# One layer of a three-branch decoder on one core: key drains moved ahead of two convolutions, a transpose moved forward, gate scalars read from PSUM

## The chip, the cores and the metric

The kernel runs on one core of a Trainium2 chip. The time is device microseconds (us) of one execution; lower is better. The engines are TensorE (PE in the profile, its weight loads PEld), VectorE (DVE), ScalarE (ACT), GpSimd (POOL) and SyncE (SP), each with a queue of its own that it works off in order.

## The reference

One layer over 512 tokens of width 1024. A combined projection feeds three token mixers (A: sparse attention over the 128 keys that a topk over index scores picks; B: gated DeltaNet; C: compressed, selected and window attention), then gates, branch projections and the output projection. The change lies in B and in C's compressed keys:

```python
g = -jnp.exp(a_log) * jax.nn.softplus(a_in + dt_bias)
g_cum = jnp.cumsum(g, axis=-1)
decay = jnp.where(lower, jnp.exp(jnp.where(lower, g_cum[..., :, None] - g_cum[..., None, :], 0.0)), 0.0)
a_mat = jnp.where(strict, jnp.einsum('bnhid,bnhjd->bnhij', k * beta, k) * decay, 0.0)
t_inv = lax.linalg.triangular_solve(eye + a_mat, eye, left_side=True, lower=True)
kc = rms_norm(compress_blocks(k_cmp, cmp_pos[0], phi_w1[0], phi_w2[0]), k_norm[0])
```

q, k and v of B pass a causal convolution of four taps and SiLU first; q and k are normalised.

## The kernel before, in words

The kernel is written engine by engine, each queue by hand; semaphores tie them together. Order of the work: x is normalised and transposed; the input projection goes through ten chunks of w_in (C0, C1, A0, QI, A2, B0, B1, B3, B4, B2; `project`, L1683 to L1685, three f16 matmuls for each f32 product); then comes B's recurrence over four token chunks c = 0 to 3, then 48 attention units u, then branch and output projections. The six gate chunks (L1979 to L1983) are no stage: `fill(n)` puts n of their matmuls wherever TensorE would wait.

**Weights.** SyncE loads a chunk in pairs of rows into three stage buffers. ScalarE scales and rounds each (`hi_split`, L740 and L748), GpSimd subtracts for the low part (`lo_split`, L528, called by `follow`), and TensorE waits for the low part. A load waits for the low part that frees its stage.

**B's inputs.** B3 brings the decay gates; B2 is the v part (features 8 to 11). `conv(m)` on VectorE (L1256, three times L1258) convolves feature m, ScalarE applies SiLU, GpSimd squares features 0 to 7 for the norms. From the gates VectorE makes the log decays g_t (L1323 to L1327); TensorE sums them (L1948, L1949, bank "sums": per token and per chunk), and GpSimd multiplies them with a triangle (`cumulative_input`, L584) for the `cumulative` matmul (L1912, bank "gc"). VectorE copies the sums into gc_, gl_ and kd_s (L1335 to L1339), subtracts (`difference(0)`, L1366), ScalarE exponentiates (`decay_exp`, L895, L896), GpSimd makes three products (`masked_decays`, L592, L595, L598), for which it also needs `key_scales` (own_root at L1038 to L1045 on 32 columns, to L1352). `decayed_products(0)` (L1379, L1381) then drains the key products kk and qk (L1881, eight matmuls each), and the first product of the inverse is L1889.

**Compressed keys.** `compressed_keys` (L1275 to L1280) norms the 31 compressed keys with own_root on one column of 31 rows; TensorE transposes them (kcT, inside B2), `twin` (L1146, L1147) drains them.

**Banks.** VectorE's two PSUM banks (`V`) are used in turn, in the order of the list v_names, and a use waits until the one two places before it is drained:

```python
v_names += list(chain(*([("ak", h)] for h in range(A_HEADS)))) + ["cmpkv", "sq", "sqT", "sums"]
v_names += [("gc", 0), ("kk", 0), ("qk", 0), "kcT", ("n", 0)]
...
def free(self, name):
    return self.at[name] + 1 - len(self.banks)
```

"sq" and "sqT" hold the square sums and their transpose (L1719, behind ScalarE's copy L901). So kcT waits for the drain of kk.

**Topk.** 96 half rounds (MAX8 at L1289, MATCH_REPLACE at L1292) over 256, 384 and then 512 scores are spread over VectorE's queue by `rounds(n)` and `between_steps`; their result is first used in unit 32. Attention units take one each.

**Waits on the same engine.** `hold` makes an engine wait for its own instruction to finish.

## Time and profile before

| | us |
|---|---|
| median of 3 runs | 604.04 (603.85 to 605.86) |
| the profiled execution | 606.39 |
| its span | 604.5 |
| TensorE busy | 548.3 (91%) |
| VectorE busy | 388.2 (64%) |
| ScalarE busy | 322.2 (53%) |
| GpSimd busy | 221.1 (37%) |

Times within the profile are microseconds from the span's start. A row of a timeline has the start, the length, the engine, the line, what is written and read, and the idle time of the engine just before it with what ended it. Matmuls are pipelined, so that a row's length is more than the spacing to the next. A TensorE clock of 1.00 is 2.4 GHz, one of 0.50 is 1.2 GHz.

### The profile page before, as it was taken

How to read it: one execution, taken by the hardware profiler on the slowest of the kernel's cores; microseconds unless marked ns; L12 is line 12 of the kernel's file. 1: busy time of each engine (PE TensorE's matmuls, PEld its weight loads, DVE VectorE, ACT ScalarE, POOL GpSimd, SP SyncE). 2: the span in 40 equal slices, each digit the busy share in tenths (PEclk: the TensorE clock that was granted, in tenths of full speed). 3: DMA queues.
4: the chain of work that ended last, by engine and by line, in shares of the span. 5: the costliest groups of instructions: out<-in, count | busy, mean ns of one | idle time of the engine just before them, and what ended most of it. 6: DMA issues, size and time to landing. Idle time of an engine off the chain costs nothing.

```text
span 604.5 us, 10710 instructions
## 1 busy us (share of the span) xinstructions
PE 548.3 (91%) x4087; PEld 306.8 (51%) x4087; DVE 388.2 (64%) x920; ACT 322.2 (53%) x573; POOL 221.1 (37%) x164
## 2 busy tenths in 40 slices
PE   2999999999999848999899998989898998899997
PEld 1544556543457423566475665545555564333443
DVE  6521397765498696777867778578896664576311
ACT  4555745356567844542624523876767675345320
POOL 0154453522046742242730712432323463234420
PEclk9999999999999997999999999999999998999999
DMA  9346865644024420220220201211221212252411
GB/s 318 109 122 155 149 107 156 206 127 117 26 54 123 121 89 2 70 72 1 75 66 3 74 32 35 72 36 36 70 71 36 71 36 69 71 210 70 140 52 53
DMA packets 31173, 52.93 MB, mean 88 GB/s; under 512 B 2743, under 2 KB 13329, under 8 KB 31121
## 3 DMA queue, kind: packets, MB, share of 16 engines
q1 hardware_dynamic: 30825, 51.68, 29.9%
q10 hardware_dynamic: 296, 0.55, 0.5%
q8 instruction: 33, 0.54, 0.4%
q14 instruction: 19, 0.16, 0.1%
HBM read 49.80 MB, written 2.42 MB: 86 GB/s over the span
## 4 chain that ended last, share of the span: by engine, by line
PE 66%; DVE 19%; ACT 7%; issue 5%; SPq 2%; DMA 1%; POOL 0%; DVEq 0%; ACTq 0%; PEldq 0%; POOLq 0%
PE bank L1683 13%; PE bank L1685 11%; PE bank L1684 11%; PE bank L1979 5%; PE bank L1981 5%; PE bank L1889 5%; PE bank L1983 5%; PE bank L1881 3%; PE bank L1719 3%; ACT stage L740 2%; PE bank L1825 2%; DVE bank L1258 1%; DVE early L1292 1%; DVE small L1289 1%; ACT late L962 1%
## 5 line engine op out<-in xcount | busy, mean ns | idle before, releaser
L528 POOL TENSOR_TENSOR w_lo<-stage,w_hi 128x1024 f16<-128x1024 f32 (+4 forms) x76 | 149.5, 1971 | 226.3 <-ACT w_hi L748 226.2
L748 ACT ACTIVATE w_hi<-stage 128x1024 f16<-128x1024 f32 (+4 forms) x76 | 74.5, 981 | 14.2 <-PE bank L1685 9.2
L1979 PE MATMUL bank<-hT_hi,w_hi 128*128 128x512 f16 x192 | 73.0, 380 | 1.7 <-PE bank L1983 0.9
L740 ACT ACTIVATE stage<-stage,small 128x512 f32<-128x512 f32 (+4 forms) x120 | 73.6, 663 | 0.5 <-DMA stage<-in_w_in 0.5
L1981 PE MATMUL bank<-hT_lo,w_hi 128*128 128x512 f16 x192 | 72.9, 380 | 0.3
L1983 PE MATMUL bank<-hT_hi,w_lo 128*128 128x512 f16 x192 | 72.8, 379 | 0.3 <-PE bank L1685 0.2
L1683 PE MATMUL bank<-w_hi,hT_hi 128*128 128x260 f16 (+4 forms) x192 | 60.9, 317 | 3.3 <-DVE hT_lo L1066 1.4
L1685 PE MATMUL bank<-w_hi,hT_lo 128*128 128x260 f16 (+4 forms) x192 | 60.8, 316 | 0.0
L1684 PE MATMUL bank<-w_lo,hT_hi 128*128 128x260 f16 (+4 forms) x192 | 60.7, 316 | 0.0
L1683 PE MATMUL bank<-hT_hi,w_hi 128*128 128x512 f16 (+1 forms) x128 | 48.1, 376 | 2.5 <-ACT work L731 1.5
L1685 PE MATMUL bank<-hT_hi,w_lo 128*128 128x512 f16 (+1 forms) x128 | 47.8, 374 | 0.0
L1684 PE MATMUL bank<-hT_lo,w_hi 128*128 128x512 f16 (+1 forms) x128 | 47.8, 374 | 0.0
L1889 PEld LDWEIGHTS bank<-work 64*64 64x64 f32 x992 | 35.5, 134 | 22.7 <-issue 11.6
L1889 PE MATMUL bank<-work 64*64 64x64 f32 x992 | 42.0, 222 | 2.8 <-DVEq L1360 2.3
L962 ACT ACTIVATE late<-late,small 128x128 f32<-128x128 f32 (+3 forms) x48 | 26.8, 557 | 27.7 <-DVE small L1469 27.6
L1390 DVE COPY_PREDICATED work<-level_masks,bank 128x256 f32<-128x256 uint8 (+1 forms) x48 | 21.3, 443 | 17.4 <-PE bank L1719 9.0
L1683 PE MATMUL bank<-strips,w_hi 128*128 128x512 f16 x64 | 25.1, 392 | 4.4 <-DVE strips L1582 1.5
L1683 PEld LDWEIGHTS bank<-w_hi,hT_hi 128*128 128x128 f16 x192 | 18.7, 98 | 19.6 <-issue 6.0
L1258 DVE SCALAR_TENSOR_TENSOR bank<-qkvT,par,bank 128x512 f32<-128x512 f32 x36 | 27.2, 755 | 1.3
L1589 DVE TENSOR_TENSOR late<-bank,late 128x128 f16<-128x128 f32 (+3 forms) x48 | 23.2, 483 | 7.1 <-ACT late L983 6.9
L1289 DVE MAX8 small<-early 128x8 f32<-128x512 f32 (+2 forms) x46 | 25.8, 561 | 2.9
L1647 DVE SCALAR_TENSOR_TENSOR late<-bank,late 128x512 f32<-128x512 f32 x8 | 5.5, 691 | 33.9 <-PE bank L1685 33.9
(331 smaller groups left out, 1139.4 us busy)
## 6 DMA issues: line engine op xcount, KB each, us to landing
stage<-in_w_in SPq DMA_DIRECT2D x40, 512.0 KB, 3.7
stage<-in_c_phi_w SPq DMA_DIRECT2D x8, 512.0 KB, 4.0
stage<-in_w_branch SPq DMA_DIRECT2D x8, 512.0 KB, 3.9
stage<-in_w_out SPq DMA_DIRECT2D x8, 512.0 KB, 4.3
stage<-in_w_in SPq DMA_DIRECT2D x8, 260.0 KB, 2.8
strips<-rel_rows SPq DMA_DIRECT2D x8, 256.0 KB, 7.1
late<-in_x SPq DMA_DIRECT2D x1, 2048.0 KB, 9.1
out_x<-late SPq DMA_DIRECT2D x8, 256.0 KB, 2.0
```

Of the source, the lines that this page charges most:

```text
L528: gp.tensor_tensor(piece_view(w_lo[:, k % PAIRS, :], c), piece_view(stage[:, piece_at[c, j] % STAGES, :], c), piece_view(w_hi[:, k % PAIRS ...
L740: ins = nc.scalar.activation(full[:, r, :], full[:, r, :], ACT.Copy, scale=g_w[:, 2 * j + r:2 * j + r + 1])
L748: nc.scalar.activation(piece_view(w_hi[:, k % PAIRS, :], c), full, ACT.Copy).then_inc(hi_ready, 1)
L962: nc.scalar.activation(probs[u % 2][:, 0:L], probs[u % 2][:, 0:L], ACT.Exp, bias=nmx[:, u:u + 1], scale=1.0 / LOGIT_SCALE, accum_out=rsum[ ...
L1258: ins = ve.scalar_tensor_tensor(acc, qkvT[:, m, w:w + T], tap[w], acc, ALU.mult, ALU.add)
L1683: mm(ps, lhs[0], rhs[0], start=start, stop=False)
L1684: mm(ps, lhs[0], rhs[1], start=False, stop=False)
L1685: return mm(ps, lhs[1], rhs[0], start=False, stop=stop)
L1889: ins = mm(ps[o:o + HALF, h * HALF:(h + 1) * HALF], lhs(h, slice(r, r + HALF)), rhs(h, slice(r, r + HALF)), start=True, stop=True)
L1979: mm(G.bank(g)[:, :], w[0], h[0], start=k == 0, stop=False)
L1981: mm(G.bank(g)[:, :], w[0], h[1], start=False, stop=False)
L1983: ins = mm(G.bank(g)[:, :], w[1], h[0], start=False, stop=k == KC - 1)
```

## The change

- VectorE: the log decays go ahead of `compressed_keys`; gc_, gl_ and kd_s are read from the bank "sums", without a copy between; `key_scales` is cut in two and goes ahead of `difference(0)`; `decayed_products(0)` goes ahead of conv(9), conv(10) and seven of the rounds, directly behind conv(8); kcT's drain goes ahead of conv(8); conv(11) goes into the first level of the inverse. The rounds move: 2, then 3, 2, 2 here, none in the first level, and two instead of one at units u with u % 4 == 2.
- TensorE: the sums' matmuls go from behind B4's last tile to ahead of it, `cumulative(0)` from inside B2 to ahead of B2, kcT from B2's third tile to its first, the key products from behind B2's second tile to behind its first, the transposes of n from the fourth tile to the second. The bank list has kcT ahead of kk.
- ScalarE: the split of B2's first pair goes from behind the softplus to ahead of the eighth SiLU.
- GpSimd: the resets go ahead of `cumulative_input(0)`, the cmp_strip copies behind the splits that follow B2.

```diff
--- before.py
+++ after.py
@@ -57,7 +57,7 @@
 
 FILL_Z, FILL_U, FILL_X, FILL_T = 7, 2, 7, 3
 
-ROUNDS_IN, ROUNDS_LOG, ROUNDS_SUM, ROUNDS_ROOT, ROUNDS_CONV = 0, 1, 1, 1, (6, 4, 3)
+ROUNDS_IN, ROUNDS_LOG, ROUNDS_CONV = 0, 2, (3, 2, 2)
 
 Y_EARLY = {34: (4,), 36: (5,), 40: (6,), 42: (7,), 46: (2,), 47: (3,)}
 Y_ORDER = (4, 5, 6, 7, 2, 3, 0, 1)
@@ -266,7 +266,7 @@
         v_names += ["cq0", "cq1", "kcmp", "vcmp", "ckvT", "aq0", "aq1"]
         v_names += [("ukv", t) for t in range(NT)] + ["ks", "kw", "kiT"]
         v_names += list(chain(*([("ak", h)] for h in range(A_HEADS)))) + ["cmpkv", "sq", "sqT", "sums"]
-        v_names += [("gc", 0), ("kk", 0), ("qk", 0), "kcT", ("n", 0)]
+        v_names += [("gc", 0), "kcT", ("kk", 0), ("qk", 0), ("n", 0)]
         for c in range(NT):
             for l in range(1, LEVELS):
                 v_names += [("z", c, l)] + ([("u", c, l)] if l < LEVELS - 1 else []) + [("ut", c, l)]
@@ -357,7 +357,6 @@
         max8 = cols(16)
         beta_t, g_t, sp_a, sp_b, neg_exp_a, dt_b = cols(16), cols(16), cols(16), cols(16), cols(4), cols(4)
         rk, nk = cols(16), cols(16)
-        sums_sb = cols(32)
         mx, nmx, rsum = cols(48), cols(48), cols(48)
         cmx, crs = cols(16), cols(16)
         fac = cols(4)
@@ -613,12 +612,16 @@
                 for m in range(4):
                     squares_b(m + 4 * (c == CH_B3))
             follow(CH_B4, 0)
-            cumulative_input(0)
             gp.memset(t_invT, 0.0)
             reset(t_h)
             reset(t_hT)
+            cumulative_input(0)
             for t in range(1, 4):
                 follow(CH_B4, t)
+            masked_decays(0)
+            follow(CH_B2, 0)
+            follow(CH_B2, 1)
+            follow(CH_B2, 2)
 
             gp.wait_ge(strips_loaded, 16 * (P // ROW_COPIES))
             for q in range(NT):
@@ -626,10 +629,6 @@
                 first = 415 - P * q
                 ins = gp.tensor_copy(cmp_strip[:, :, q, 0:n], strips[:, A_HEADS:, first:first + 16 * (n - 1) + 1:16])
             ins.then_inc(cmp_strip_ready, 1)
-            masked_decays(0)
-            follow(CH_B2, 0)
-            follow(CH_B2, 1)
-            follow(CH_B2, 2)
 
             def scaled_output(c):
 
@@ -878,6 +877,7 @@
             silu_conv(2)
             drain_chunk(CH_B3, "B3", lambda t: raw_b[:, t, 0:260], 260, between=lambda t: silus(t, {0: (3,), 1: (4,), 2: (5,), 3: (6,)}))
 
+            hi_split(CH_B2, 0)
             silu_conv(7)
             drain(("B4", 0), raw_b[:, 0, 260:520], 260, scale=1.0 / W_SCALE)
             act.wait_ge(s_drained, S.filled(("B3", 3)))
@@ -895,7 +895,6 @@
                 hold(nc.scalar.activation(decay, decay, ACT.Relu, scale=-1.0))
                 nc.scalar.activation(decay, decay, ACT.Exp, scale=-1.0).then_inc(exp_ready, 1)
 
-            hi_split(CH_B2, 0)
             drain(("B4", 1), raw_b[:, 1, 260:520], 260, scale=1.0 / W_SCALE)
             act.wait_ge(v_filled, V.filled("sq"))
             nc.scalar.activation(sum_rows, V.bank("sq")[:, :], ACT.Copy).then_inc(v_drained, 1)
@@ -1316,7 +1315,6 @@
             hold(ve.scalar_tensor_tensor(sp_b, sp_a, -1.0, sp_a, ALU.mult, ALU.max))
             hold(ve.tensor_scalar(sp_a, sp_a, 0.0, None, ALU.max))
             ve.nop().then_inc(GATE_IN.sem, 1)
-            compressed_keys()
             rounds(ROUNDS_LOG)
             GATE_OUT.wait(ve, "sp")
             for g in (beta_t, raw_c1[:, :, 192:204]):
@@ -1326,17 +1324,15 @@
             hold(ve.tensor_tensor(gt, sa, neg_exp_a.unsqueeze(1).to_broadcast([P, NT, 4]), ALU.mult))
             hold(ve.tensor_scalar(g_t, g_t, -1.0, None, ALU.mult))
             ve.nop().then_inc(gsum_ready, 1)
-            rounds(ROUNDS_SUM)
-            rounds(ROUNDS_ROOT)
+            compressed_keys()
             ve.tensor_copy(ss_b.rearrange("p (a t h) -> p t h a", a=2, t=NT),
                            filled("sqT")[:, :].rearrange("p (t h n) -> p t h n", t=NT, h=4)[:, :, :, 0:2]).then_inc(v_drained, 1)
             ve.wait_ge(v_drained, V.filled("sqT"))
             ps = filled("sums")
-            ve.tensor_copy(sums_sb, ps[:, 0:32]).then_inc(v_drained, 1)
+            hold(ve.tensor_copy(gc_, ps[:, 0:16]))
+            ve.tensor_copy(gl_, ps[:, 16:32])
+            ve.tensor_tensor(kd_s, ps[:, 16:32], gc_, ALU.subtract).then_inc(v_drained, 1)
             ve.wait_ge(v_drained, V.filled("sums"))
-            ve.tensor_copy(gc_, sums_sb[:, 0:16])
-            ve.tensor_copy(gl_, sums_sb[:, 16:32])
-            hold(ve.tensor_tensor(kd_s, sums_sb[:, 16:32], sums_sb[:, 0:16], ALU.subtract))
             ve.nop().then_inc(GATE_IN.sem, 1)
 
             def key_scales():
@@ -1347,6 +1343,8 @@
                 hold(ve.tensor_tensor(a_s, beta_t, rk, ALU.mult))
                 hold(ve.scalar_tensor_tensor(n_s, a_s, -1.0, rk, ALU.mult, ALU.mult))
                 ve.nop().then_inc(scales_ready, 1)
+
+            def decay_scales():
                 GATE_OUT.wait(ve, "exps")
                 ve.tensor_scalar(negegc, egc, -1.0, None, ALU.mult)
                 hold(ve.tensor_tensor(kd_s, ekd, rk, ALU.mult))
@@ -1468,18 +1466,18 @@
                 ve.wait_ge(v_drained, V.filled(("lg", m, q, h)))
                 ve.tensor_scalar(nmx[:, u:u + 1], mx[:, u:u + 1], -1.0 / LOGIT_SCALE, None, ALU.mult).then_inc(logits_ready, 1)
 
+            key_scales()
             difference(0)
-            key_scales()
+            twin("kcT", kcT[:, 0, 0:N_CMP], kcT[:, 1, 0:N_CMP], R_CK, N_CMP)
+            decay_scales()
+            conv(8)
+            decayed_products(0)
             rounds(ROUNDS_CONV[0])
-            conv(8)
+            level_zero(0)
             rounds(ROUNDS_CONV[1])
             conv(9)
-            decayed_products(0)
-            twin("kcT", kcT[:, 0, 0:N_CMP], kcT[:, 1, 0:N_CMP], R_CK, N_CMP)
             rounds(ROUNDS_CONV[2])
-            level_zero(0)
             conv(10)
-            conv(11)
             for c in range(NT):
                 norm = output_norm(c - 1) if c else iter(())
                 softmax = compressed_softmax() if c == NT - 1 else iter(())
@@ -1487,6 +1485,9 @@
 
                 def between_steps(l, late_in_level=False):
 
+                    if (c, l, late_in_level) == (0, 1, False):
+                        conv(11)
+                        return
                     if l < 3 or next(extras, "end") == "end":
                         rounds(1)
                         if not late_in_level:
@@ -1601,7 +1602,7 @@
                     for _ in norm:
                         pass
                 elif u < 28:
-                    rounds(1)
+                    rounds(2 if u % 4 == 2 else 1)
                 for f in Y_EARLY.get(u, ()):
                     y_lo(f)
                 if u % 4 == 3 and u >= 7:
@@ -1942,23 +1943,22 @@
                 if t == 2:
                     pe.wait_ge(v_drained, V.filled("sq"))
                     transposes("sqT", [sum_rows[:, t * P:(t + 1) * P] for t in range(NT)])
-                if t == 3:
                     pe.wait_ge(gsum_ready, 1)
                     ps = v_bank("sums")
                     mm(ps[:, 0:16], tri, g_t, start=True, stop=True)
                     mm(ps[:, 16:32], ones[:, :], g_t, start=True, stop=True).then_inc(v_filled, 1)
+                if t == 3:
+                    cumulative(0)
 
             def between_b2(t):
-                if t == 1:
+                if t == 0:
                     key_products(0)
 
             def within_b2(t, k):
                 if (t, k) == (0, 2):
-                    cumulative(0)
-                if (t, k) == (2, 1):
                     T_IN.wait(pe, "kc")
                     transposes("kcT", [raw_c0[0:N_CMP, 0, 0:128]], N_CMP)
-                if (t, k) == (3, 1):
+                if (t, k) == (1, 6):
                     GD.wait(pe, ("nnt", 0))
                     transposes(("n", 0), [neg_nT[:, h, :] for h in range(4)])
```

Line numbers of the changed kernel are one to three lower on VectorE from L1289 on, and one higher on TensorE. Three places, before and after, each as the queue has them.

TensorE, from the transposes of the square sums (sqT) to the first matmuls of B2. Before, the last rows of B4 and the first of B2:

```order
L1684 MATMUL bank<-w_lo,hT_hi 128x260
L1685 MATMUL bank<-w_hi,hT_lo 128x260
L1948 MATMUL bank<-small,consts 128x16
L1949 MATMUL bank<-small,ones 128x16
L1683 MATMUL bank<-hT_hi,w_hi 128x512
L1684 MATMUL bank<-hT_lo,w_hi 128x512
L1685 MATMUL bank<-hT_hi,w_lo 128x512
L1683 MATMUL bank<-hT_hi,w_hi 128x512
```

Now:

```order
L1686 MATMUL bank<-w_hi,hT_lo 128x260
L1720 MATMUL bank<-consts,early 128x128 x4
L1948 MATMUL bank<-small,consts 128x16
L1949 MATMUL bank<-small,ones 128x16
L1684 MATMUL bank<-w_hi,hT_hi 128x260
L1685 MATMUL bank<-w_lo,hT_hi 128x260
```

and at B4's end:

```order
L1685 MATMUL bank<-w_lo,hT_hi 128x260
L1686 MATMUL bank<-w_hi,hT_lo 128x260
L1913 MATMUL bank<-work,ones 128x512
L1684 MATMUL bank<-hT_hi,w_hi 128x512
L1685 MATMUL bank<-hT_lo,w_hi 128x512
L1686 MATMUL bank<-hT_hi,w_lo 128x512
L1684 MATMUL bank<-hT_hi,w_hi 128x512
```

L1948 and L1949 are the sums; they stood behind B4 and are now ahead of its last tile. L1913 is the cumulative matmul (L1912 before), now the first thing behind B4.

VectorE, from the end of the key scales to the first copies for the inverse. Before:

```order
L1256 TENSOR_SCALAR bank<-qkvT,par 128x512
L1258 SCALAR_TENSOR_TENSOR bank<-qkvT,par,bank 128x512 x3
L1292 MATCH_REPLACE early<-small,early 128x256
L1289 MAX small<-early 128x8
L1292 MATCH_REPLACE early<-small,early 128x256
L1289 MAX small<-early 128x8
L1256 TENSOR_SCALAR bank<-qkvT,par 128x512
L1258 SCALAR_TENSOR_TENSOR bank<-qkvT,par,bank 128x512 x3
L1379 TENSOR_TENSOR work<-bank,late 128x512
L1381 TENSOR_TENSOR work<-bank,work 128x512
L1390 COPY_PREDICATED work<-level_masks,work 64x256 x2
L1146 TENSOR_SCALAR kcT<-bank,par 128x31
```

Now:

```order
L1364 TENSOR_TENSOR work<-bank,g_scale 128x512
L1145 TENSOR_SCALAR kcT<-bank,par 128x31
L1146 SCALAR_TENSOR_TENSOR kcT<-bank,par,kcT 128x31
L1349 TENSOR_SCALAR g_scale<-g_scale 128x16
L1350 TENSOR_TENSOR g_scale<-g_scale,small 128x16
L1255 TENSOR_SCALAR bank<-qkvT,par 128x512
L1257 SCALAR_TENSOR_TENSOR bank<-qkvT,par,bank 128x512 x3
L1377 TENSOR_TENSOR work<-bank,late 128x512
L1379 TENSOR_TENSOR work<-bank,work 128x512
L1388 COPY_PREDICATED work<-level_masks,work 64x256 x2
L1288 MAX small<-early 128x8
```

L1379 and L1381 (now L1377 and L1379) are the key drains, L1256 and L1258 (L1255, L1257) one convolution, L1146 (L1145) the drain of kcT. Two convolutions and ten rounds stood ahead of the key drains, now one convolution does, and kcT is drained ahead of it.

GpSimd, from the split of B2's first pair on. Before:

```order
L528 TENSOR_TENSOR w_lo<-stage,w_hi 128x1024
L584 TENSOR_TENSOR work<-consts,small 128x512
L617 MEMSET work 128x512
L587 COPY work<-consts 128x256 x2
L528 TENSOR_TENSOR w_lo<-stage,w_hi 128x1024 x3
L627 COPY cmp_strip<-strips 128x4x7
L627 COPY cmp_strip<-strips 128x4x15
L627 COPY cmp_strip<-strips 128x4x23
L627 COPY cmp_strip<-strips 128x4x31
L592 TENSOR_TENSOR work<-work,consts 128x512
L595 TENSOR_TENSOR late<-work,g_scale 128x512
L598 TENSOR_TENSOR work<-work,small 128x512
```

Now:

```order
L527 TENSOR_TENSOR w_lo<-stage,w_hi 128x1024
L615 MEMSET work 128x512
L586 COPY work<-consts 128x256 x2
L583 TENSOR_TENSOR work<-consts,small 128x512
L527 TENSOR_TENSOR w_lo<-stage,w_hi 128x1024 x3
L591 TENSOR_TENSOR work<-work,consts 128x512
L594 TENSOR_TENSOR late<-work,g_scale 128x512
L597 TENSOR_TENSOR work<-work,small 128x512
L527 TENSOR_TENSOR w_lo<-stage,w_hi 128x1024 x4
L630 COPY cmp_strip<-strips 128x4x7
```

L584 (L583) is the cumulative input, L592 to L598 (L591 to L597) are the masked decays, L528 (L527) the splits. The cumulative input now stands behind the resets, the masked decays directly behind B2's splits.

## Rows read from the trace of the kernel before

**Rows 1.** the page, part 4: the chain that ended last, shares by engine
```profile
PE 66%; DVE 19%; ACT 7%; issue 5%; SPq 2%; DMA 1%; POOL 0%; DVEq 0%; ACTq 0%; PEldq 0%; POOLq 0%
```

**Rows 2.** windows: length, each engine's busy time (instructions), granted clock, DMA share, GB/s
```profile
200.00:220.00 20.00, 17.95 (x101) 9.85 (x98) 15.20 (x38) 16.63 (x25) 15.78 (x17) 1.00 0.37 106
220.00:240.00 20.00, 11.39 (x43) 4.99 (x44) 13.88 (x29) 5.16 (x9) 3.39 (x2) 0.74 0.19 53
```

**Rows 3.** TensorE's timeline: start us, length us, engine, line, operation, [idle before <-releaser]
```profile
199.38 0.66 PE L1719 MATMUL bank<-consts,early 128*128 128x128 f32 x4 [1.77 <-ACT early L901]
...
205.73 1.02 PE L1912 MATMUL bank<-work,ones 128*128 128x512 f32 x2
...
209.24 0.39 PE L1683 MATMUL bank<-hT_hi,w_hi 128*128 128x512 f16 x1 [0.55 <-POOL w_lo L528]
...
218.59 0.38 PE L1685 MATMUL bank<-hT_hi,w_lo 128*128 128x512 f16 x1
...
228.61 0.28 PE L1719 MATMUL bank<-consts,early 31*128 31x31 f32 x1 [9.64 <-DVE work L1379]
...
234.22 0.38 PE L1684 MATMUL bank<-hT_lo,w_hi 128*128 128x512 f16 x1
...
236.60 0.60 PE L1719 MATMUL bank<-consts,work 128*128 128x128 f32 x4
...
241.39 0.68 PE L1889 MATMUL bank<-work 64*64 64x64 f32 x16 [0.30 <-PE bank L1685]
```

**Rows 4.** VectorE's timeline, the gate scalars to the first key drain
```profile
203.71 0.19 DVE L1335 COPY small<-bank 128x32 f32<-128x32 f32 x1 [3.35 <-PE bank L1949]
203.94 1.12 DVE L1337 COPY g_scale<-small 128x16 f32<-128x16 f32 x1
...
207.05 2.18 DVE L1339 TENSOR_TENSOR g_scale<-small 128x16 f32<-128x16 f32 x1
...
211.53 1.31 DVE L1045 TENSOR_TENSOR small<-small 128x32 f32<-128x32 f32 x1
...
215.27 0.19 DVE L1348 SCALAR_TENSOR_TENSOR g_scale<-g_scale,small 128x16 f32<-128x16 f32 x1
...
220.53 2.34 DVE L1258 SCALAR_TENSOR_TENSOR bank<-qkvT,par,bank 128x512 f32<-128x512 f32 x3
...
227.78 0.68 DVE L1379 TENSOR_TENSOR work<-bank,late 128x512 f32<-128x512 f32 x1
```

**Rows 5.** GpSimd's timeline, 202 to 218 us
```profile
202.88 6.30 POOL L528 TENSOR_TENSOR w_lo<-stage,w_hi 128x1024 f16<-128x1024 f32 x3
...
211.52 1.27 POOL L592 TENSOR_TENSOR work<-work,consts 128x512 f32<-128x512 f32 x1 [1.35 <-ACT work L896]
...
216.67 1.04 POOL L598 TENSOR_TENSOR work<-work,small 128x512 f32<-128x512 f32 x1
```

**Rows 6.** timeline of all engines at 291 us
```profile
291.04 2.13 POOL L528 TENSOR_TENSOR w_lo<-stage,w_hi 128x1024 f16<-128x1024 f32 x1 [0.17 <-ACT w_hi L748]
...
291.26 1.92 DVE L1028 TENSOR_TENSOR small<-small 128x4 f32<-128x4 f32 x1
```

**Rows 7.** ScalarE's timeline, 191 to 197 us
```profile
191.99 0.60 ACT L866 ACTIVATE qkvT<-bank 128x512 f32<-128x512 f32 x1 [2.50 <-DVE bank L1258]
...
196.16 1.32 ACT L740 ACTIVATE stage<-stage,small 128x512 f32<-128x512 f32 x2
```

**Rows 8.** VectorE's timeline, first and last of the 19 compressed-key instructions
```profile
193.89 0.21 DVE L1275 TENSOR_TENSOR early<-early 31x64 f32<-31x64 f32 x1
...
197.06 0.40 DVE L1280 TENSOR_SCALAR early<-early,small 31x64 f32<-31x64 f32 x2
```

**Rows 9.** windows in the attention stage, columns as in rows 2
```profile
410.00:420.00 10.00, 9.69 (x80) 5.66 (x77) 8.60 (x33) 5.17 (x17) 1.12 (x2) 1.00 0.19 54
430.00:440.00 10.00, 9.06 (x87) 5.60 (x88) 9.37 (x31) 7.88 (x19) 2.83 (x2) 1.00 0.04 15
```

**Rows 10.** VectorE's timeline in attention, a topk round
```profile
432.08 0.68 DVE L1289 MAX8 small<-early 128x8 f32<-128x512 f32 x1
```

## The prediction

> **What bounds the kernel now.** The page comes first. The chain that ended last runs on TensorE for 66% of the span, on VectorE for 19% [rows 1]: time goes where TensorE idles or runs slowly. The windows show where: in 220:240 TensorE is busy 11.39 of 20 us and its mean granted clock is 0.74; in the 20 us before, 17.95 us at 1.00 [rows 2]. TensorE's timeline gives the two parts of that hole [rows 3]. After the matmul at 218.59 nothing runs until the key transpose (kcT) at 228.61: 9.64 us, released by VectorE's L1379. Then the transpose and 13 matmuls fill 228.61 to 234.22, 5.6 us at 1.2 GHz, where the next 11 fill 234.22 to 236.60 at 2.4 GHz: 0.216 us each, so the 14 would take 3.0 us and the slow clock costs 2.6 us.
>
> VectorE's timeline says why L1379 is late [rows 4]. kcT writes the bank that ("kk", 0) filled, and L1379 drains that bank. Ahead of it in VectorE's queue: the gate scalars from 203.71, three 16-column writes that end only at 209.23, the decay difference, the key scales (210.21 to 215.46), ten rounds of topk, and conv(8) and conv(9), each 2.34 us for three of its four instructions, 3.1 in all.
>
> **Collisions.** The three 16-column writes take 1.12, 2.18 and 2.18 us, though such an instruction takes 0.19 (the one at 215.27) [rows 4]. Meanwhile GpSimd runs three splits back to back, 202.88 to 209.18, 2.1 us each, and each write ends as a split ends [rows 4, 5]. The same holds for L1045 at 211.53, 1.31 us beside the mask product that ends at 212.79, and for a multiply of four columns, L1028, that begins 0.2 us into a split and lasts 1.92 us [rows 5, 6]. The copy out of PSUM at 203.71 takes 0.19 us inside a split: not caught [rows 4]. So here a small VectorE operation from SBUF to SBUF waits for GpSimd's running operation; one with its input in PSUM doesn't.
>
> **The change, step by step** (times of the profiled execution).
>
> 1. ScalarE's split of B2's first pair (2.3 us from 196.16 on) moves into the 2.50 us for which ScalarE waits before 191.99 [rows 7]: no cost. ScalarE's copy of the square sums behind it (L901) comes 2.3 us earlier, and TensorE's 1.77 us wait for it before 199.38 goes [rows 3].
>
> 2. gc_, gl_ and kd_s come from PSUM: 203.71 to 209.23 (5.5 us) becomes about 0.6 us.
>
> 3. The log decays go ahead of the compressed keys. Softplus is there at 196.2; five small operations, two or three of them beside GpSimd's resets, end at about 197.7. Then come the compressed keys: 19 instructions, 193.89 to 197.4, 3.5 us with GpSimd idle [rows 8]. **Now GpSimd isn't idle.** It runs the cumulative input (about 1.0 us), then the three splits, each when ScalarE has its high part: 2.3 us apiece behind the copy of the square sums (done at 199.3 before, so at 197.0 now), with drains between, so splits at about 199.3, 201.9 and 204.4. Ten of the 19 are products of two SBUF operands. If each is caught as the 128-row ones are, the chain waits 1.0 us for the cumulative input and 1.7, 2.0 and 2.1 us for the splits: 197.8 + 3.5 + 6.8 = 208.1. Bounds: 201.3 if nothing is caught; 208.5 if every one is. No row has a 31-row operation beside a GpSimd operation; the nearest, four columns caught for 1.92 us [rows 6], is why I take 208.1.
>
> The Trainium skill (SBUF — State Buffer, Who interferes with whom) says that a VectorE operation with two SBUF inputs contends with a GpSimd operation that reads SBUF, that the later one blocks fully, and that one with at most one SBUF input outside the two-port modes doesn't contend; by it the sum is the one with 208.1, and the trace agrees for 128 rows.
>
> 4. TensorE: the sums' matmuls move to before B4's last tile, the cumulative matmul to behind it, ahead of the 9 matmuls (1.9 us) that it followed; with the 1.77 us gone it could start at 205.73 - 1.9 - 1.8 = 202.0. But it needs the bank of sqT, which VectorE drains only behind the compressed keys, at 208.3. A wait of about **6.4 us in front of B2** takes the place of the 9.64 us inside it.
>
> 5. From the cumulative matmul on, before needed 241.39 - 205.73 = 35.66 us to the first inverse product [rows 3]. Less 9.64, 2.6 and 0.55 (the weight wait at 209.24), plus the 9 matmuls of B2 that were ahead of it (1.9): 24.8 us. So 208.4 + 24.8 = 233.2 in place of 241.39: **-8.2 us**.
>
> Does something else stop TensorE there? Key scales 208.8 to 213.0 (5.25 less the collision's 1.1), difference 213.8, kcT drained 214.3; TensorE asks for that bank at 214.6. Margin 0.3 us, thin. ScalarE's two decay operations end at 215.1, GpSimd's three products at 218.5 (1.27 and twice 1.04) [rows 5], kk is drained at 219.3, wanted at 220.9: 1.6 us. conv(11) in place of two rounds in the first level: a copy and 3.1 us beside 13 fill matmuls (2.8 us) and the u and ut products: hidden. The cmp_strip copies move behind B2's splits, nobody waits. SyncE's loads follow the splits; its queue changes nowhere.
>
> 6. The clock. Before, it fell within 9.64 us of idleness and came back after 5.4 us of work. Nothing shows what 6.4 us do. I take the same **+2.6**, bounds 0 and 2.6: a shorter wait shouldn't cost more.
>
> 7. Topk rounds. Ahead of the first inverse product 16 become 9, two in the first level give way to conv(11), and nine more run in attention, where a round takes some 0.7 us (0.68 the instruction [rows 10]): one more at units 2, 6, 10, 14, 18 and 22, one at 25 and two at 26, which had none. Early there VectorE has room (8.60 of 10 us busy, TensorE 9.69); in 430:440 it has hardly any (9.37, TensorE 9.06) [rows 9], and about four of the nine fall there, less the slack behind. I take **+2**, bounds 0 and 6.5.
>
> 8. The recurrence: cheaper topk forms on VectorE, but collisions such as L1028's fall anew. 0, bounds -1.5 and +1.5.
>
> Sum: -8.2 + 2.6 + 2.0 = -3.6. The profiled execution took 606.39 us (span 604.5); the median of the runs is 604.04. So 602.8 on the profiled execution's scale, **600.4** on the median's.
>
> **Rivals.**
> - *No collision for 31 rows.* The keys are ready at 201.3, the cumulative matmul starts at 202.0, no long wait, no fall of the clock: 202.0 + 24.8 = 226.8, -14.6, +2 for the rounds: 591.4. For it: no row has the case, and one-column operations move few bytes. Against it: four columns were caught just as long as sixteen.
> - *The same wait, no fall of the clock:* 597.8. It lies in my forecast's own range.
> - *VectorE becomes the bound behind B2 (slower).* 3.1 us of conv(11) and nine rounds of 0.7, less two cheap rounds, move behind the first inverse product: 8.4 us. If attention, already at 94% of VectorE in 430:440, and the recurrence pass all of it on: -5.6 + 8.4 = +2.8, 606.8. It decides from 7.4 us on. Against it: TensorE is 97% busy in 410:420 and VectorE has 14% free there.
> - *The hole only moves.* The wait for sqT grows to the old 9.6 us or the thin margin breaks, and attention takes the rest: within 1.8 us of before, about 604.
>
> **Chances.** A difference of 0.3% (1.8 us) is about what a measurement of this kernel can tell. The forecast (with or without the clock) 0.57; no or few collisions 0.23; hole only moves 0.10; VectorE bound 0.10. The forecast's terms span 594 to 604.5; a fifth of its chance lies within 0.3%, a little above it. Faster 0.23 + 0.45 = 0.68, rounded up for the mixed cases to 0.7; same 0.17; slower 0.13. Range 589.5 to 604.5: it takes in the first rival and leaves out the slower end. The likeliest is 600.4.
>
> **What will show it.** VectorE's L1041, L1042 or L1044 on 31 rows with 1.5 to 2.1 us beside GpSimd's splits, and TensorE idle 5 to 7 us before the cumulative matmul (L1913), released by the copy of sqT (L1328): right. Those at 0.15 us and no such gap: the first rival. L1332 to L1334 at about 0.2 us each: step 2. No TensorE wait above 1 us within B2: step 5. PEclk below 1 right after the gap: step 6. TensorE idle growing in the attention units: step 7; by over 6 us, the slower rival. I am wrong at the root if TensorE waits in B2 for L1377 or for ScalarE's drains.

## The result and the profile after

The changed kernel takes **607.29 us** (median of 7 runs, 606.76 to 607.64) beside 604.04 (7 runs, 602.63 to 605.96): ratio 1.0047, 95% interval 1.0029 to 1.0065. It is slower by half a per cent. Forecast were 600.4 us and a range of 589.5 to 604.5: the direction is wrong and the time lies outside the range. On the chips of the later experiments the kernel before has a median of 605.7 to 606.0 us, and its single executions there differ: those with a mean granted clock of 0.991 took 602.9 to 604.2 us, those with 0.986 took 605.5 to 607.1. The changed kernel wasn't run beside these (against them 607.29 would be 0.2 to 0.3% slower), so the size of its loss is less sure than its direction.

The span of the profiled execution is 605.5 us (604.5 before). The spans differ by less than the medians, as the execution profiled before took 606.39 us, 2.35 above its median, and the one after is its kernel's median. The stage in which the change gained, columns as in [rows 2]:

```profile
200.00:220.00 20.00, 13.23 (x63) 6.91 (x62) 15.34 (x47) 10.56 (x17) 9.58 (x7) 0.83 0.27 79
220.00:240.00 20.00, 19.70 (x135) 9.60 (x134) 16.81 (x32) 12.04 (x18) 10.28 (x9) 1.00 0.37 106
```

The hole of [rows 2, 3] in 220:240 is gone and a smaller one stands in 200:220. TensorE's timeline shows it, in front of the cumulative matmul instead of the key transpose:

```profile
208.09 2.05 PE L1913 MATMUL bank<-work,ones 128*128 128x512 f32 x2 [6.77 <-DVE small L1328]
```

VectorE's timeline says why the copy of sqT (L1328) is late: the compressed keys on 31 rows, and gate scalars that now cost nothing.

```profile
197.86 1.11 DVE L1274 TENSOR_TENSOR early<-early 31x64 f32<-31x64 f32 x1
...
199.78 2.00 DVE L1041 TENSOR_TENSOR small<-small 31x1 f32<-31x1 f32 x1
...
202.35 2.01 DVE L1041 TENSOR_TENSOR small<-small 31x1 f32<-31x1 f32 x1
...
204.75 1.91 DVE L1044 TENSOR_TENSOR small<-small 31x1 f32<-31x1 f32 x1
...
207.75 0.19 DVE L1328 COPY small<-bank 128x32 f32<-128x32 f32 x1
207.98 0.19 DVE L1332 COPY g_scale<-bank 128x16 f32<-128x16 f32 x1
...
208.29 0.18 DVE L1334 TENSOR_TENSOR g_scale<-bank,g_scale 128x16 f32<-128x16 f32 x1
```

GpSimd's timeline has the operations that hold them ("held" here: the VectorE operation takes long beside a GpSimd operation and ends with it). The first is the cumulative input, the others are splits:

```profile
197.86 1.04 POOL L583 TENSOR_TENSOR work<-consts,small 128x512 f32<-128x512 f32 x1 [0.68 <-DVEq L1326]
199.64 2.13 POOL L527 TENSOR_TENSOR w_lo<-stage,w_hi 128x1024 f16<-128x1024 f32 x1 [0.74 <-ACT w_hi L747]
202.22 2.13 POOL L527 TENSOR_TENSOR w_lo<-stage,w_hi 128x1024 f16<-128x1024 f32 x1 [0.46 <-ACT w_hi L747]
204.54 2.12 POOL L527 TENSOR_TENSOR w_lo<-stage,w_hi 128x1024 f16<-128x1024 f32 x1 [0.18 <-ACT w_hi L747]
```

The front of the kernel went nearly as forecast, then. Where the gain went is seen by the starts of the attention units' transposes (120 matmuls: first and last start). Before, then after:

```profile
L2112 PE MATMUL bank<-consts,late x120: 271/273/330, 389.7 to 502.1; 128*128 128x128 f32 x120
```

```profile
L2112 PE MATMUL bank<-consts,late x120: 272/273/421, 381.4 to 504.8; 128*128 128x128 f32 x120
```

The account of the span (profiled executions; the first inverse product starts at 241.4 before [rows 3] and 234.8 after):

| stretch | before, us | after, us | difference |
|---|---|---|---|
| start to first inverse product | 241.4 | 234.8 | -6.6 |
| to the first attention transpose | 148.3 | 146.6 | -1.7 |
| **attention transposes, first to last** | **112.4** | **123.4** | **+11.0** |
| to the end | 102.4 | 100.7 | -1.7 |
| span | 604.5 | 605.5 | +1.0 |

At the door of the attention stage the changed kernel leads by 8.3 us. It loses 11.0 us there: TensorE is idle for 15.4 us of the stage instead of 8.6, and its busy time is 108.0 us instead of 103.8. (The last -1.7 is a spell of half clock in 500:520, mean 0.91, so 1.8 us lost, that this execution of the kernel before had and the one after lacks.) In the middle of the stage TensorE is emptier than before, VectorE a little fuller (the time for which an operation is held counts as busy), and the granted clock falls. Before, then after:

```profile
400.00:420.00 20.00, 19.39 (x146) 11.17 (x143) 16.01 (x64) 12.10 (x38) 5.13 (x3) 1.00 0.19 54
420.00:440.00 20.00, 17.70 (x147) 10.27 (x147) 16.73 (x57) 15.54 (x35) 7.11 (x4) 1.00 0.18 53
440.00:460.00 20.00, 18.61 (x174) 11.38 (x173) 17.21 (x54) 13.34 (x30) 3.01 (x2) 1.00 0.18 54
```

```profile
400.00:420.00 20.00, 16.99 (x129) 9.72 (x128) 17.60 (x56) 11.85 (x30) 5.00 (x3) 1.00 0.10 27
420.00:440.00 20.00, 15.79 (x122) 8.88 (x121) 17.42 (x53) 11.59 (x30) 4.99 (x3) 0.94 0.28 79
440.00:460.00 20.00, 16.87 (x143) 10.13 (x142) 17.78 (x50) 10.98 (x23) 2.13 (x1) 0.89 0.09 28
```

Means of 0.94 and 0.89 over 20 us are together 6.8 us at half clock. In windows of half a microsecond TensorE is busy for all of it (437.6 to 441.0 and 451.3 to 454.7), so up to 3.4 us are lost. TensorE's timeline has three waits of over 2 us for L1590 (VectorE's low half of the transposed probabilities) where the kernel before has none above 1.0 in this part:

```profile
405.29 0.19 PE L1684 MATMUL bank<-v_c,late 128*128 128x64 f16 x1 [2.36 <-DVE late L1590]
...
436.69 0.19 PE L1684 MATMUL bank<-v_c,late 128*128 128x64 f16 x1 [2.31 <-DVE late L1590]
...
450.07 0.19 PE L1684 MATMUL bank<-v_c,late 128*128 128x64 f16 x1 [2.58 <-DVE late L1590]
```

Ahead of each, VectorE's timeline shows the same thing: a topk half round, then a group's finish (L1560 to L1574), whose product of the reciprocals with the gates (L1562, 128 x 4) is held. The first and the third of them, and the splits beside them:

```profile
399.81 0.68 DVE L1291 MATCH_REPLACE8 early<-small,early 128x512 f32<-128x512 f32 x1
400.52 0.18 DVE L1560 RECIPROCAL small<-small 128x4 f32<-128x4 f32 x1
400.73 1.99 DVE L1562 TENSOR_TENSOR small<-small,raw_c 128x4 f32<-128x4 f32 x1
...
445.30 1.66 DVE L1562 TENSOR_TENSOR small<-small,raw_c 128x4 f32<-128x4 f32 x1
```

```profile
400.57 2.13 POOL L527 TENSOR_TENSOR w_lo<-stage,w_hi 128x1024 f16<-128x1024 f32 x1 [5.67 <-ACT w_hi L747]
...
444.82 2.13 POOL L527 TENSOR_TENSOR w_lo<-stage,w_hi 128x1024 f16<-128x1024 f32 x1 [8.89 <-ACT w_hi L747]
```

With the one at 432.47 (1.70) that is 1.82 + 1.53 + 1.49 = 4.8 us more than three free ones of 0.17. Before, the longest of the eight takes 0.52. But it was close there too: the three products that belong to these begin 0.22, 0.28 and 0.21 us ahead of a split, where they now begin 0.16, 0.46 and 0.48 us behind one. The third of them before:

```profile
446.15 0.17 DVE L1561 TENSOR_TENSOR small<-small,raw_c 128x4 f32<-128x4 f32 x1
...
446.36 2.28 POOL L528 TENSOR_TENSOR w_lo<-stage,w_hi 128x1024 f16<-128x1024 f32 x1 [6.48 <-ACT w_hi L748]
```

**Theory A:** TensorE waits for VectorE in the attention units, and nine added half rounds (33 in the stage instead of 24), three held finishes and the clock spells behind TensorE's waits make the 11 us. **Rival B:** the stage starts 8.3 us earlier and waits for something else that is late. **Rival D:** the rounds alone do it, wherever the splits fall. The experiments below name the ratio to the kernel before, measured on the same chip, and "stage" is the first to the last start of the 120 transposes as above.

### The profile page after: what moved, and what is told of

Its sections match the earlier page's. It is cut to its first block, busy times and chain, and to the rows that moved or that the text cites. A ratio compares the mean times of both kernels' runs of the same rounds, so it can differ in the third digit from the quotient of the medians.

```text
span 605.5 us, 10706 instructions
## 1 busy us (share of the span) xinstructions
PE 550.3 (91%) x4087; PEld 308.6 (51%) x4087; DVE 393.8 (65%) x919; ACT 321.9 (53%) x573; POOL 221.3 (37%) x164
## 4 chain that ended last, share of the span: by engine, by line
PE 68%; DVE 18%; ACT 6%; issue 5%; SPq 2%; DMA 1%; POOL 0%; DVEq 0%; ACTq 0%; PEldq 0%; POOLq 0%
PE bank L1684 13%; PE bank L1686 12%; PE bank L1685 12%; PE bank L1890 5%; PE bank L1979 5%; PE bank L1981 5%; PE bank L1983 4%; PE bank L1882 4%; PE bank L1720 2%; PE bank L1826 2%; DVE late L1464 2%; DVE early L1291 1%; ACT stage L739 1%; DVE late L1590 1%; ACT late L961 1%
## 5 line engine op out<-in xcount | busy, mean ns | idle before, releaser
L527 POOL TENSOR_TENSOR w_lo<-stage,w_hi 128x1024 f16<-128x1024 f32 (+4 forms) x76 | 149.3, 1966 | 217.3 <-ACT w_hi L747 217.3
L1257 DVE SCALAR_TENSOR_TENSOR bank<-qkvT,par,bank 128x512 f32<-128x512 f32 x36 | 27.2, 756 | 1.3
L1590 DVE TENSOR_TENSOR late<-bank,late 128x128 f16<-128x128 f32 (+3 forms) x48 | 23.2, 483 | 7.1 <-ACT late L982 6.9
```

What stands on the lines that cost most here:

```text
L527: gp.tensor_tensor(piece_view(w_lo[:, k % PAIRS, :], c), piece_view(stage[:, piece_at[c, j] % STAGES, :], c), piece_view(w_hi[:, k % PAIRS ...
L1590: ve.tensor_tensor(probsT[u % 2][:, 1, 0:L], S.bank(("pT", m, q, h))[:, 0:L], probsT[u % 2][:, 0, 0:L], ALU.subtract).then_inc(s_drained, 1)
```

## Experiments on the attention stage

**Single rounds again, seven rounds put into VectorE's idle time ahead of conv(8)** (run of the changed kernel with):

```
-ROUNDS_IN, ROUNDS_LOG, ROUNDS_CONV = 0, 2, (3, 2, 2)
+ROUNDS_IN, ROUNDS_LOG, ROUNDS_SLOT, ROUNDS_CONV = 0, 2, 6, (3, 2, 3)
             decay_scales()
+            rounds(ROUNDS_SLOT)
             conv(8)
-                    rounds(2 if u % 4 == 2 else 1)
+                    rounds(1)
```

> The changed kernel with one topk half round per attention unit again, and seven half rounds of the first query tile more in the idle 3.01 us that VectorE has ahead of conv(8) (217.47) and behind it. Theory A (VectorE bounds the attention stage; nine added rounds of 0.7 us, three collisions of 1.5 to 1.8 us in the group finishes and two spells of the half clock made it 11.0 us longer): the first inverse product stays at 234.8 within 1 us, TensorE's waits for L1590 fall from 10.8 to under 5 us, the stage shortens by 6 to 11 us: 596 to 601 us. Rival B (the stage is longer because it starts 8.3 us earlier and meets something else late, a drained gate or a split weight): the stage hardly shortens, 605 to 608 us.

Measured: **598.42 us, ratio 0.9870 (0.9846 to 0.9895)**. The first inverse product starts at 235.1, 0.3 us later than in the changed kernel, and the half clock ahead of it cost 0.9 us more here (last section), so the seven rounds cost nothing there. The stage takes 112.7 us. TensorE's waits for L1591 (the same operation) in 395:520 come to 3.6 us; they were 10.8 in the changed kernel and 3.8 in the kernel before (us in all, times, longest):

```profile
PE bank L1685 <- DVE late L1591: 3.6, 6, 1.5
```

Rival B is out: the stage starts at 382.0, as early as in the changed kernel, and is as short as before.

**Step 7 alone in the kernel before:**

```
-ROUNDS_IN, ROUNDS_LOG, ROUNDS_SUM, ROUNDS_ROOT, ROUNDS_CONV = 0, 1, 1, 1, (6, 4, 3)
+ROUNDS_IN, ROUNDS_LOG, ROUNDS_SUM, ROUNDS_ROOT, ROUNDS_CONV = 0, 1, 1, 1, (3, 2, 1)
-                    rounds(1)
+                    rounds(2 if u % 4 == 2 else 1)
```

> The kernel before with step 7 alone: seven half rounds less ahead of the convolutions and in them (3.3 us of VectorE, which the key drain of the third tile waits for), nine attention rounds in the doubled places (two of which stay empty). Theory A: the hole before 228.61 shrinks by about 3 us and attention grows by 5 (seven rounds of 0.7 us) to 9 us (with new collisions): 606 to 610 us. Rival B (the rounds themselves are nearly free in attention): 601 to 602.5 us.

Measured: **611.31 us, ratio 1.0088 (1.0062 to 1.0113)**, a little beyond the expected end. (The profiled execution was the slowest of the six, 613.18 us.) The gap before the key transpose shrinks from 9.64 to 7.21, and the first inverse product comes 2.5 us earlier (238.9). Only seven more half rounds run in the stage here (31). It takes 121.7 us, 9.3 more, with the same waits:

```profile
410.94 0.19 PE L1683 MATMUL bank<-v_c,late 128*128 128x64 f16 x1 [2.37 <-DVE late L1589]
...
442.33 0.19 PE L1683 MATMUL bank<-v_c,late 128*128 128x64 f16 x1 [2.31 <-DVE late L1589]
455.73 0.19 PE L1683 MATMUL bank<-v_c,late 128*128 128x64 f16 x1 [2.57 <-DVE late L1589]
```

The loss in attention belongs to the moved rounds and not to the rest of the change. Rival B is out by this as well: the stage starts at 387.8 here.

**Reciprocals written to PSUM,** into unused columns of the group's output bank, so that L1562's product has one SBUF input:

```
+                recip = O.bank(("o", m, q))[:, 256:260] if m != "A" else fac
-                hold(ve.reciprocal(fac, rsum[:, 4 * g:4 * g + 4]))
+                hold(ve.reciprocal(recip, rsum[:, 4 * g:4 * g + 4]))
-                    hold(ve.tensor_tensor(fac, fac, gate[...], ALU.mult))
+                    hold(ve.tensor_tensor(fac, recip, gate[...], ALU.mult))
```

(both behind the wait for the group's output)

> The changed kernel with the reciprocals of the row sums written to PSUM, so that the product with the gates (L1562) has one SBUF input. If a VectorE operation with two SBUF inputs is what GpSimd's splits hold up, none of the six such products takes more than 0.3 us (they took up to 1.99, 1.70 and 1.66), TensorE's waits at 405.29, 436.69 and 450.07 fall by about 1.5 us each and the total by 3 to 5 us, 602 to 604 (up to 6 if a clock spell goes too). If the rounds alone do it (rival D), the waits are eaten elsewhere: 606 to 608.

Measured: **603.95 us, ratio 0.9973 (0.9958 to 0.9987)**, stage 119.1. All eight products take 0.16 or 0.17, inside a split too, but at two finishes the copy behind the product is held in its place. So of TensorE's three waits only the second shrinks as expected (0.78); the first and the third stay at 2.17 and 2.38:

```profile
401.07 0.17 DVE L1564 TENSOR_TENSOR small<-bank,raw_c 128x4 f32<-128x4 f32 x1
401.27 1.91 DVE L1572 COPY work<-work 128x256 f32<-128x256 f32 x1
...
442.94 1.53 DVE L1572 COPY work<-work 128x256 f32<-128x256 f32 x1
```

**The copy taken out as well** (the first product adds the compressed output directly, the sum is the same):

```
-                elif m == "sel":
-                    hold(ve.tensor_copy(oc, o_cg[:, 4 * q:4 * q + 4, :]))
+                        more = o_cg[:, 4 * q + h, :] if m == "sel" else oc[:, h, :]
```

> The changed kernel, doubled rounds kept, with reciprocals in PSUM and without the copy: no operation of the group finishes is left that a split holds up (in the run with the reciprocals alone the copy was held for 1.91 and 1.53 us). This prices the nine rounds alone: the attention stage 115 to 118 us (123.4 in the changed kernel, 119.1 with the reciprocals alone, 112.7 without the doubled rounds), total 600 to 603. If something else is caught in the copy's place, it stays at 119 and 604.

Measured: **598.99 us, ratio 0.9900 (0.9881 to 0.9919)**, stage 114.9, both just below what I expected. All nine rounds are still there. The waits for L1590 above 0.7 us are now four of 0.75 to 0.87 and the one behind the stage (1.51), which the kernel before has as well; the clock is 1.00 in every window of 380:500.

**The same two edits in the kernel before,** as the control:

> The kernel before with the reciprocals in PSUM and without the copy of the compressed output. Its finishes met no split worth naming (0.52 us at most), so the edit should give nothing but four copies of 0.29 us and that one: 604 to 606 us beside 605.8, ratio 0.997 to 1.000. If it gives 4 us or more here too, what it gave in the changed kernel (8.3 us) is the edit's own and not the price of new collisions.

Measured: **603.68 us, ratio 0.9972 (0.9959 to 0.9985)**, stage 111.0 (112.4 before). The edits are worth 1.4 us of the stage by themselves, where nothing is held. So of the 8.5 us they gave in the changed kernel (123.4 to 114.9) **7.1 are the price of the held finishes with the clock spells behind the waits**, and 114.9 - 111.0 = **3.9 us are the price of nine more rounds**. Together 11.0. TensorE's busy time divides the 7.1. With the edits its idle time in the stage falls from 15.4 to 10.0 us in the changed kernel and from 8.6 to 7.4 before, its busy time from 108.0 to 104.9 and from 103.8 to 103.6: so 4.2 us are idle time and 2.9 are slower work, which fits the up to 3.4 us of the half clock.

With the finishes freed in both kernels, the change gives what was forecast: 0.9900 / 0.9972 = 0.993, some 4 us faster, beside a forecast of 3.6.

**The second round in another unit:**

```
-                    rounds(2 if u % 4 == 2 else 1)
+                    rounds(2 if u % 4 == 0 else 1)
```

> The changed kernel with the second half round given to units 4, 8, 12, 16, 20 and 24 instead of 2, 6, 10, 14, 18 and 22: as many rounds in attention, but not in the unit ahead of a group's finish. If the loss is the number of rounds (about 3 us, and only with collisions 11), the splits may meet other finishes: 600 to 607 us, and each us above 600 is there as a held operation (1.5 to 2 us each) in the list of L1562 and of the copy. If the doubled place itself makes the loss, 598 to 601 with no operation held. If it is the count alone whatever is held, 606 to 608 as in the changed kernel.

Measured: **602.43 us, ratio 0.9945 (0.9926 to 0.9965)**, stage 116.7, with as many rounds as in the changed kernel. The longest L1562 takes 0.52, no copy over 0.30, the clock stays at 1.00 in 380:500. How near a miss this is the timelines of VectorE and GpSimd show:

```profile
400.68 0.30 DVE L1571 COPY work<-work 128x256 f32<-128x256 f32 x1
...
440.64 0.29 DVE L1571 COPY work<-work 128x256 f32<-128x256 f32 x1
```

```profile
400.72 2.24 POOL L527 TENSOR_TENSOR w_lo<-stage,w_hi 128x1024 f16<-128x1024 f32 x1 [5.70 <-ACT w_hi L747]
...
440.69 2.23 POOL L527 TENSOR_TENSOR w_lo<-stage,w_hi 128x1024 f16<-128x1024 f32 x1 [7.22 <-ACT w_hi L747]
```

The copies begin 0.04 and 0.05 us ahead of a split, and here the split takes 0.1 us longer instead. In the changed kernel L1562 begins 0.16 us behind one and takes 1.99. Rival D is out: as many rounds, and 6.7 us less in the stage than in the changed kernel. The run with the product and the copy freed says the same with the rounds left in their places. The expected second case (598 to 601 us, no loss at all) is out too, and of the first only the time is met, as no operation is held: what is left over the 112.7 us of single rounds, 4.0 us, is the price of the rounds again.

## Experiments on the front

**The compressed keys back ahead of the log decays:**

```
+            compressed_keys()
             rounds(ROUNDS_LOG)
...
             ve.nop().then_inc(gsum_ready, 1)
-            compressed_keys()
```

> The changed kernel with the compressed keys back ahead of the log decays. If the collisions with GpSimd's cumulative input and splits made the keys late (5.8 us of waiting in them), none of L1274, L1041, L1044 on 31 rows takes over 0.5 us, TensorE's wait of 6.77 us before the cumulative matmul falls under 1.5 us, the clock doesn't fall there, and the first inverse product comes at 226 to 230 instead of 234.8; the total drops by 5 to 9 us, 598 to 602, if attention doesn't take it back. Rival C (TensorE would only wait further on, for the drains of kk and qk): the product at 232 or later, 605 to 607 us.

Measured: **604.72 us, ratio 0.9981 (0.9966 to 0.9997)**, between the two cases. The first inverse product comes at 231.0 instead of 234.8, and the attention stage keeps its loss (122.4). The 6.77 us are gone, but not all of it is gained. TensorE waits 3.10 us for the log decays ahead of the sums' matmuls; one of the keys' operations is held once (L1274, 1.99, by the split at 193.42); and the three splits now meet the key scales:

```profile
202.26 1.83 DVE L1037 TENSOR_SCALAR small<-small 128x32 f32<-128x32 f32 x1
204.12 2.05 DVE L1038 TENSOR_SCALAR small<-small 128x32 int32<-128x32 int32 x1
206.21 2.05 DVE L1039 TENSOR_SCALAR small<-small 128x32 int32<-128x32 int32 x1
```

**Step 2 alone in the kernel before** (gc_, gl_ and kd_s read from PSUM, nothing else):

> The kernel before with step 2 alone (gate scalars read from PSUM). L1332 to L1334 take 0.2 us each instead of 1.1 to 2.2. Theory A (what GpSimd's splits hold up is whatever SBUF to SBUF operation comes next): the key scales behind them are caught instead, the key drain L1379 comes earlier by 0 to 2 us only, 603 to 606 us. Rival E (the gain of 4.9 us counted in step 2 is real by itself): 599 to 602 us.

Measured: **604.64 us, ratio 0.9981 (0.9966 to 0.9996)**: 1.1 us of the 4.9. The three writes take 0.18 each, and VectorE then waits for the next thing and is held elsewhere:

```profile
204.31 0.18 DVE L1337 TENSOR_TENSOR g_scale<-bank,g_scale 128x16 f32<-128x16 f32 x1
207.08 0.69 DVE L1365 TENSOR_TENSOR work<-bank,g_scale 128x512 f32<-128x512 f32 x1 [2.59 <-PE bank L1911]
207.92 1.63 DVE L1038 TENSOR_SCALAR small<-small 128x32 f32<-128x32 f32 x1
```

The next thing is TensorE's cumulative matmul (2.59 us), which was hidden behind the held writes; held in their place are the first of the key scales (1.63) and, at 210.82, a product of them (1.14).

**What a split cannot hold, put beside the splits.** Single attention rounds; keys ahead of the log decays; the sums' matmuls behind B4's last tile; and ten of the 16 rounds ahead of the first inverse product between the sums' drain and the key scales (of the edit, the lines on these):

```
-ROUNDS_IN, ROUNDS_LOG, ROUNDS_CONV = 0, 2, (3, 2, 2)
+ROUNDS_IN, ROUNDS_LOG, ROUNDS_SPLIT, ROUNDS_CONV = 0, 0, 10, (2, 2, 2)
+            rounds(ROUNDS_SPLIT)
             key_scales()
             difference(0)
...
-                    rounds(2 if u % 4 == 2 else 1)
+                    rounds(1)
```

> One round per attention unit; compressed keys ahead of the log decays, the sums' matmuls behind B4's last tile instead of ahead of it, and ten topk rounds (which GpSimd doesn't hold up) between the sums' drain and the key scales, in the time in which the splits held up the key scales in the run with the early keys. If collisions and attention rounds are separate costs that add up: TensorE waits under 1.5 us before the sums, no clock spell behind them, the first inverse product comes at 227 to 230 (234.8 in the changed kernel), the attention stage stays at 112 to 114 us, total 592 to 596. If the key drains bind instead (conv(8) later by what the rounds cost), the product comes at 231 or later and the total is 596 to 599.

Measured: **598.69 us, ratio 0.9900 (0.9876 to 0.9924)**, first product at 232.2. That is the expected second case for the front and the total. The stage is a miss (112 to 114 expected): it takes 116.3, since with this start one finish meets a split again (L1563, 1.99 us at 435.80, and TensorE waits 2.58 behind it), though every unit has a single round.

**The same with the finishes freed** (reciprocals in PSUM, no copy, as above):

> The same with the reciprocals in PSUM and without the copy of the compressed output (the first product adds it directly): with single rounds the finishes met no split worth naming (0.52 us at most), so only the four copies of 0.29 us go: within 1.5 us of the run above. If attention is still bound by VectorE, up to 3 us less.

Measured: **594.72 us, ratio 0.9832 (0.9808 to 0.9855)**, stage 111.6: 4 us less than the run before and outside what I expected, as one finish had been held there (the stage is 4.7 us shorter). The rounds beside the splits (201.27 to 207.58) run at full speed, all ten of this form:

```profile
206.38 0.43 DVE L1288 MAX8 small<-early 128x8 f32<-128x256 f32 x1
...
206.92 0.41 DVE L1291 MATCH_REPLACE8 early<-small,early 128x256 f32<-128x256 f32 x1
207.36 0.26 DVE L1037 TENSOR_SCALAR small<-small 128x32 f32<-128x32 f32 x1
...
212.46 2.47 PE L1883 MATMUL bank<-qkvT 128*128 128x128 f32 x16 [3.36 <-DVE work L1364]
```

The last row (TensorE's) is the wait that was left: L1364, the decay difference. **The difference ahead of the key scales** (against the run just before):

```
-            rounds(ROUNDS_SPLIT)
-            key_scales()
-            difference(0)
+            rounds(ROUNDS_SPLIT // 2)
+            difference(0)
+            rounds(ROUNDS_SPLIT // 2)
+            key_scales()
```

> The version of the second group without the copy (594.7 us) with the decay difference between the first and the last five of the ten rounds, ahead of the key scales instead of behind them. If TensorE's 3.36 us before 212.46 are the wait for the drain of the cumulative sums' bank by it (L1364), they fall under 1 us and the first inverse product comes at 229 to 230.5 instead of 232.5, 591 to 594 us in all. If VectorE's own queue binds (the key drains), the wait only moves behind it: 594 to 596.

Measured: **595.09 us, ratio 0.9835 (0.9815 to 0.9856)**: nothing. The first inverse product even comes 1.6 us later (234.1). The wait only moved, to the key transpose's drain behind the key scales:

```profile
214.02 1.23 PE L1884 MATMUL bank<-qkvT 128*128 128x128 f32 x4 [4.00 <-DVE kcT L1146]
```

**That drain moved up too,** to directly behind the difference:

> The version of the third group with the difference first (595.1 us), and the key transpose's drain (kcT) also ahead of the second five rounds and the key scales. Its TensorE wait of 4.00 us before 214.02 was released by that drain (L1146). If it was only the order in VectorE's queue, the wait falls under 1 us, the first inverse product comes 2.5 to 4 us earlier and the total is 591 to 593. If VectorE's whole queue up to the drains of kk and qk binds, the product moves less than 1.5 us and the total stays at 594 to 595.5.

Measured: **592.42 us, ratio 0.9770 (0.9749 to 0.9790)**. The first inverse product comes at 229.8 (234.1 in the run before it), a wait of 2.68 us is left at 217.89, and the clock is 1.00 in 200:220. This version beats both kernels: by 2.3% the kernel before and by some 2.8% the changed one (by the ratios; the two weren't run side by side).

## Why the prediction was wrong, step by step

- **Step 1** right: in 190:240 TensorE's only wait above 0.3 us is the 6.77.
- **Step 2** right in size (0.19, 0.19, 0.18), but by itself worth 1.1 us: behind the held writes stood the wait for TensorE's cumulative matmul, and the key scales as the next to be held.
- **Step 3** right, and the choice between its bounds too: products of two operands on 31 rows are held as on 128; 1.11, 2.00, 2.01 and 1.91 us, keys ready at about 207.8 (208.1 forecast). The rival without collisions (591.4) is out.
- **Step 4** right: 6.77 us (6.4).
- **Steps 5 and 6**: -8.2 + 2.6 forecast for the first inverse product, -6.6 measured. From the cumulative matmul at 208.09 (208.4) it took 26.7 us. The mean of 0.83 over 200:220 is 6.8 us at half clock, but it began at 205.5, while TensorE waited, and only the 4.2 us from 208.09 to 212.3 met work: it cost 2.1 us, within the bounds of 0 and 2.6. The rest took 24.6 (24.8). Both margins held: no wait for L1377 or the kcT drain.
- **Step 8**: the recurrence gave 1.7 us, just beyond the bound of 1.5.
- **Step 7 is the one that failed**: "+2, bounds 0 and 6.5" for the attention stage, which lost 11.0. The nine rounds alone cost 3.9 and lie in the bounds. What was missing is 7.1 us. I had allowed for new collisions in step 8, in the recurrence only, though attention has the same pair: GpSimd's splits, and L1561 with two SBUF inputs in each finish. And I had tied a fall of the clock to the 6.4 us wait alone; two waits of 2.31 and 2.58 us in attention are each followed by one. The second round, in the unit ahead of each finish, moved three finishes from 0.2 to 0.3 us ahead of a split to behind its start. I also took 14% of free time in a window as cover; that a unit's chain (probabilities, their low half, the output product) has no use for time that is free elsewhere in the window is my reading of why 3.9 us were not covered, and no run tests it.
- **The slower rival** (606.8, chance 0.10) named the right place and, to 0.5 us, the time. Its sum was right by luck: 8.4 us for rounds and conv(11), where the rounds cost 3.9, conv(11) nothing that shows (the recurrence gained), and held operations and clock made up the rest. Its point of decision (7.4 us) is met: attention and recurrence together took back 9.3.
- **Sum and range.** By the profiled spans the forecast was -3.6 and the result +1.0. The 4.6 us between them are +9.0 (step 7), -1.0 (steps 5 and 6), -1.7 (step 8) and -1.7 (the half clock behind attention in the execution profiled before, which has no term). The range was also drawn too narrow by its own terms: -8.2 + 2.6 + 6.5 + 1.5 is +2.4, so 606.4, where I wrote 604.5. The time lies outside that too.

Step 3 cited the Trainium skill (SBUF — State Buffer, Who interferes with whom) for operations with two SBUF inputs. The same section also names those in a two-port mode. No run shows the mode of an operation, but some with one SBUF input are held: the copy once the product's input was in PSUM (1.91 us), and TENSOR_SCALARs on 128 x 32 in the early-keys run (2.05 us). Others aren't: MAX8, MATCH_REPLACE8, the reciprocal on 128 x 4 (0.18 us at 445.09) and a TENSOR_SCALAR on 31 x 1 (0.14 us at 204.58), both inside a split. I applied the section to the front only.

**Open:** what makes the clock fall. A wait of 2.36 us at 405.29, one of 2.58 at 446.29 in the early-keys run and one of 2.68 at 217.89 in the last version have no half clock behind them (1.00 in their windows), those of 2.31 and 2.58 in the changed kernel have. In the kernel before a wait of only 1.51 us, at 505.82, has one behind it, from 507.2 on. That the spells in attention come from the held finishes rests on this: of the five kernels in which a held finish makes TensorE wait 2.3 us or more, four have such a spell in 380:480, and of the nine others none has.

## What to carry to other kernels

A held operation is not a cost at its place but a property of what runs beside GpSimd: make one cheap and the next that can be held is held, so fill such a stretch with operations that weren't held in any run (here ten topk rounds), or give the exposed ones a PSUM input. Before moving work into a later stage, walk through that stage's chain with each operation that can be held and ask where it lands against each GpSimd operation; here shifts of 0.4 to 0.7 us decided over 1.5 to 1.8 us each time. And a gain ahead of a stage is worth nothing until the work pushed into it is priced there.

## What was not expected of the hardware

- Two TensorE waits as short as 2.31 and 2.58 us are each followed by matmuls at half clock (128 x 512, f16: 0.63 us instead of 0.38), from 437.6 on, 0.9 us behind the end of the first wait:

```profile
437.38 0.41 PE L1979 MATMUL bank<-hT_hi,w_hi 128*128 128x512 f16 x1
...
438.22 0.63 PE L1981 MATMUL bank<-hT_lo,w_hi 128*128 128x512 f16 x1
438.64 0.63 PE L1983 MATMUL bank<-hT_hi,w_lo 128*128 128x512 f16 x1
```

- The same wait in front (6.75 to 6.78 us in five kernels) is not followed by the same spell. At work TensorE spent 4.2 us at half clock behind it in the changed kernel, 6.0 in the run with single rounds and 5.7, 3.7 and 5.0 in the runs with the product freed, with the copy out as well and with the second round in another unit: 1.8 to 3.0 us lost. A single profile can't fix such a term to better than about 1 us.
- Where a finish's copy begins at most 0.06 us ahead of a split, the split takes 2.23 to 2.28 us instead of 2.13 (nine cases in five kernels, the kernel before among them): being held works both ways.
